# A split-precision decoder trunk: the activation's two parts meet the weight's high part in one 512-column matmul

## The chip, the cores and the metric

The kernel runs on one core of one Trainium2 chip. The metric is the device time of one execution in microseconds (us). A change of about 1% (some 8 us here) is what a measurement of this kernel can just tell from no change.

## The reference

One sequence of 256 tokens with 1024 features goes through two layers. Layer 0 mixes tokens with RWKV-7 time mixing, layer 1 with native sparse attention (compressed, selected and sliding-window branches); each is followed by a dense MLP with a squared ReLU. Everything is float32.

```
def squared_relu_mlp(x, w1, w2):
    return jnp.square(jax.nn.relu(x @ w1)) @ w2          # 1024 -> 4096 -> 1024

for i in range(DEPTH):                                   # DEPTH = 2
    xn = rms_norm(h, mix_norm[i])
    y = rwkv7_time_mix(xn, ...) if i % 2 == 0 else nsa_mix(xn, ...)
    h = h + y                                            # y ends in "@ w_out", 1024 -> 1024
    h = h + squared_relu_mlp(rms_norm(h, mlp_norm[i]), mlp_w1[i], mlp_w2[i])
```

## The kernel before

Activations are held transposed: features on the 128 partitions, 256 tokens (T) along the free axis, eight tiles of 128 features (FT). A dense layer is computed in float32r, the one-pass form of a float32 matmul, which keeps fewer bits of its operands. To keep accuracy every operand is split in two: the weight `raw` into `whi` (its rounded part) and `wlo` (the rest), the activation into a high and a low tile (`xh`/`xl`, `yh`/`yl`, `hh`/`hl`). Three of the four products are added in PSUM: whi times high, whi times low, wlo times high.

Weights are streamed from HBM in 188 units of 512 KB. A unit holds four tiles of 128 input features by 256 output features (`UE` = 1024 values per partition), and lies in one of four slots (`RING`). Each unit goes through four steps:

1. SyncE issues its DMA into `raw` once the slot's former unit has been split (`load`, and the loops in `mlp_loads`).
2. ScalarE copies `raw` to `whi` (`split`, line 1124; `split_of`, line 1359), once TensorE is done with the slot (`unit_used`).
3. VectorE subtracts, `raw` - `whi` gives `wlo` (`rest`, line 1530, reached through `ahead` as well).
4. TensorE runs `unit_mm` (line 454): per input tile k three products, for each of the unit's two output tiles m, so 24 matmuls of 128x128 weights and 256 columns. Output tiles m = 0 and 1 lie in two neighbouring PSUM banks.

Two units make a group, which is a complete result of 256 output features when the layer has 1024 inputs (`a2` and `b2`, with 4096 inputs, take eight units to a group). Groups alternate between banks 0-1 and banks 2-3, so a bank pair has to be emptied before the second next group (`group_free`).

The dense layers, in the order in which they run, are `r`, `k`, `v` (inputs of RWKV, 8 units each), `o0` (its output, 8), `a1` and `a2` (MLP of layer 0, 32 each), `kc`, `ks`, `q`, `vv` (inputs of attention, 20 in all), `o1` (8), `b1` and `b2` (MLP of layer 1, 32 each). The order of the instructions on each engine is the order of the Python code; nothing is rescheduled.

How groups are emptied, in the layers that the change touches:

- `o0`, `a2`, `o1`, `b2`: VectorE adds a bank pair to the residual stream, `h += ps` (`add_residual`, line 1566). Where a norm follows (`residual`), ScalarE then writes `xh` (line 1156) and VectorE `xl` (line 1573) for the next layer, and both gather the squares (`sqn`, lines 1159 and 1579). The next layer's first unit can start while the last two feature pairs are being made: `parts` lets it wait for each pair by itself. After the first group of `a1` or `b1` TensorE takes the mean of the squares (`mean_pe`, line 494), ScalarE its root, VectorE the reciprocal `ri`.
- `a1`, `b1`: VectorE computes `rl` = max(ps, 0) times `ri` (line 1867), which frees the banks; ScalarE squares it into `hh` (line 1363), VectorE squares it into `s2` (line 1870), splits the next two units (line 1530, twice), and writes `hl` = `s2` - `hh` (line 1877). `mlp_dve` and `mlp_act` hold this turn, 16 of them in each MLP.

At the end TensorE transposes `h` (line 1100) and two DMAs store it.

## Time and profile before

| | us |
|---|---|
| median of 3 runs | 777.41 |
| the runs | 769.60, 777.41, 778.11 |
| profiled execution, its own time | 770.58 |
| span of the profiled execution | 768.5 |
| TensorE busy, matmuls | 740.7 (96%) |
| TensorE busy, weight loads | 695.2 (90%) |
| VectorE busy | 520.1 (68%) |
| ScalarE busy | 379.2 (49%) |

The span runs from the first to the last recorded instruction; the profiled execution took 2.1 us more. PE is TensorE's matmuls, PEld its weight loads, which overlap the matmuls, DVE is VectorE, ACT ScalarE, POOL GpSimd, SP SyncE. The duration of one matmul or weight load in a row is its latency; since such instructions overlap, the rate is read from the distance between starts. A true float32 matmul shows as two records (two passes), a float32r one as one record. In "x2" rows of a timeline two equal instructions are merged.

### The profile page before, as it was taken

Reading aid. Unit: us, or ns where it says so; the run is one execution under the profiler, and the core shown is the slowest. Engines: PE = TensorE matmul, PEld = TensorE weight load, DVE = VectorE, ACT = ScalarE, POOL = GpSimd, SP = SyncE. Lnnn points to the kernel's source line nnn. Section 1 sums busy time; section 2 is a strip of 40 time slices with the busy share of each in tenths; the row PEclk is TensorE's granted clock in tenths of the full one; section 3 lists DMA queues with packets and bytes.
Section 4 is the critical chain, followed back from the end, with each engine's and each line's share of the span. In section 5 each row is a group of like instructions: output and inputs, shape, how many; then the busy total and the mean of one; then the engine's idle time right before and its main releaser. Section 6 shows DMA issues by size and latency. Waiting matters only on the chain.

```text
span 768.5 us, 18778 instructions
## 1 busy us (share of the span) xinstructions
PE 740.7 (96%) x7940; PEld 695.2 (90%) x7940; DVE 520.1 (68%) x742; ACT 379.2 (49%) x584; POOL 70.5 (9%) x50
## 2 busy tenths in 40 slices
PE   7999999998999999999999999988899999999997
PEld 6988888997879999999999989866589999999997
DVE  4896985677453788785555678687858887864441
ACT  6656453211443545544444435668866544543341
POOL 0000005190130000000000010024420000000000
PEclk9999999999999999999999999999999999999999
DMA  9854330000111589967666553500045666676551
GB/s 294 272 174 137 96 101 26 5 3 2 58 57 55 165 233 237 241 191 225 193 197 193 169 165 112 164 1 2 1 147 166 203 196 191 191 218 194 191 165 55
DMA packets 110894, 109.24 MB, mean 142 GB/s; under 512 B 7120, under 2 KB 109776, under 8 KB 110704
## 3 DMA queue, kind: packets, MB, share of 16 engines
q1 hardware_dynamic: 110832, 108.34, 46.9%
q8 instruction: 48, 0.79, 0.4%
q14 instruction: 14, 0.11, 0.0%
HBM read 107.28 MB, written 1.05 MB: 141 GB/s over the span
## 4 chain that ended last, share of the span: by engine, by line
PE 84%; DVE 8%; SPq 2%; ACT 2%; DMA 1%; issue 1%; POOL 1%; ACTq 0%; DVEq 0%; POOLq 0%
PE ps L454 64%; PE ps L670 4%; DMA raw<-in_rwkv_w_in 1%; DVE Gs L1715 1%; DVE SB L2057 1%; PE ps L767 1%; PE ps L982 1%; PE ps L569 1%; PE ps L971 1%; PE ps L1001 1%; PE ps L756 1%; DVE nmx L2063 1%; DVE LT L1741 1%; PE ps L552 1%; POOL t L2126 1%
## 5 line engine op out<-in xcount | busy, mean ns | idle before, releaser
L1530 DVE TENSOR_TENSOR wlo<-raw,whi 128x1024 fp32r<-128x1024 f32 x188 | 226.1, 1225 | 88.8 <-ACT whi L1124 86.5
L1124 ACT ACTIVATE whi<-raw 128x1024 fp32r<-128x1024 f32 x124 | 130.3, 1058 | 128.1 <-PE ps L454 122.4
L454 PE MATMUL ps<-xh,whi 128*128 128x256 f32 x896 | 178.1, 280 | 2.7 <-DVE wlo L1530 1.1
L454 PE MATMUL ps<-xl,whi 128*128 128x256 f32 x896 | 175.4, 277 | 0.0
L454 PE MATMUL ps<-xh,wlo 128*128 128x256 f32 x896 | 175.2, 277 | 0.0
L454 PEld LDWEIGHTS ps<-xh,whi 128*128 128x128 f32 x896 | 135.4, 188 | 6.8 <-issue 4.3
L454 PEld LDWEIGHTS ps<-xl,whi 128*128 128x128 f32 x896 | 135.5, 188 | 0.0
L454 PEld LDWEIGHTS ps<-xh,wlo 128*128 128x128 f32 x896 | 135.4, 188 | 0.0
L1359 ACT ACTIVATE whi<-raw 128x1024 fp32r<-128x1024 f32 x64 | 68.0, 1063 | 78.0 <-PE ps L454 59.2
L454 PE MATMUL ps<-hl,whi 128*128 128x256 f32 x512 | 99.8, 276 | 0.0
L454 PE MATMUL ps<-hh,whi 128*128 128x256 f32 x512 | 99.6, 276 | 0.0
L454 PE MATMUL ps<-hh,wlo 128*128 128x256 f32 x512 | 99.6, 276 | 0.0
L454 PEld LDWEIGHTS ps<-hl,whi 128*128 128x128 f32 x512 | 77.2, 188 | 0.0
L454 PEld LDWEIGHTS ps<-hh,whi 128*128 128x128 f32 x512 | 77.0, 188 | 0.0
L454 PEld LDWEIGHTS ps<-hh,wlo 128*128 128x128 f32 x512 | 77.0, 188 | 0.0
L1867 DVE SCALAR_TENSOR_TENSOR rl<-ps,ri 128x512 f32<-128x512 f32 x32 | 22.1, 691 | 30.3 <-PE ps L454 29.9
L670 PEld LDWEIGHTS ps<-DP,LT 64*64 64x64 f32 x1024 | 30.7, 135 | 3.8 <-DVE DP L1746 2.6
L670 PE MATMUL ps<-DP,LT 64*64 64x64 f32 x1024 | 31.8, 219 | 1.9 <-DVE DP L1733 0.9
L2176 POOL TENSOR_TENSOR SB<-SB,cof 128x512 f32<-128x512 f32 (+1 forms) x16 | 24.4, 1524 | 78.3 <-DVE cof L2079 78.1
L1566 DVE TENSOR_TENSOR h<-h,ps 128x512 f32<-128x512 f32 x16 | 11.0, 688 | 29.6 <-PE ps L454 27.1
L1288 ACT ACTIVATE DP<-ps 128x512 f32<-128x512 f32 x16 | 9.6, 597 | 35.8 <-PE ps L670 35.8
L1870 DVE TENSOR_TENSOR s<-rl 128x512 f32<-128x512 f32 x32 | 22.2, 692 | 1.1
(308 smaller groups left out, 974.6 us busy)
## 6 DMA issues: line engine op xcount, KB each, us to landing
raw<-in_mlp_w SPq DMA_DIRECT2D x128, 512.0 KB, 4.5
raw<-in_rwkv_w_in SPq DMA_DIRECT2D x24, 512.0 KB, 5.1
raw<-in_nsa_w_in SPq DMA_DIRECT2D x20, 512.0 KB, 4.7
raw<-in_rwkv_w_out SPq DMA_DIRECT2D x8, 512.0 KB, 3.4
raw<-in_nsa_w_out SPq DMA_DIRECT2D x8, 512.0 KB, 3.5
cw<-in_nsa_cmp_w SPq DMA_DIRECT2D x4, 512.0 KB, 9.1
cst<-in_consts SPq DMA_DIRECT2D x1, 1047.0 KB, 11.3
xtok<-in_x SPq DMA_DIRECT2D x2, 512.0 KB, 4.2
```

Of the source, the lines that this page charges most:

```text
L454: last = mm(ps[:, bank0 + m, 0:T], w[:, slot, c0:c0 + P], x_[:, kk, :], start=(kk == 0 and n == 0), stop=(kk == ktiles - 1 and n == 2))
L552: last = mm(ps[:, 4 + 2 * (k % 2) + i, 0:T], lup[half, k * P:(k + 1) * P], hwa[half, :], start=True, stop=True)
L569: last = mm(ps[0:width, bank, 0:T], ldown[:, k, c0:c0 + width], mixg[:, k, :], start=(k == 0), stop=(k == FT - 1))
L670: last = mm(ps[at(e), bank, p * C:(p + 1) * C], lhs[s][at(e), p, :], DP[s][at(e), p, which, :], start=True, stop=True)
L1124: A(whi[:, s, :], raw[:, s, :], ACT.Copy).then_inc(hi_ready, 1)
L1288: A(dst, ps[:, bank, :].rearrange("p (k n) -> p k n", n=C), ACT.Copy).then_inc(sem(f"inv_act{s}"), 1)
L1359: A(whi[:, 2 * gg + j, :], raw[:, 2 * gg + j, :], ACT.Copy).then_inc(hi_ready, 1)
L1530: v.tensor_tensor(wlo[:, slot, :], raw[:, slot, :], whi[:, slot, :].bitcast(f32), ALU.subtract)\
L1566: v.tensor_tensor(h[:, 2 * g:2 * g + 2, :], h[:, 2 * g:2 * g + 2, :], ps[:, 2 * (g % 2):2 * (g % 2) + 2, 0:T], ALU.add).then_inc(ev_dve, 1)
L1867: v.scalar_tensor_tensor(rl[:, gg, :, :], ps[:, 2 * gg:2 * gg + 2, 0:T], 0.0, normal(2), ALU.max, ALU.mult)\
L1870: v.tensor_tensor(s2[:, gg, :, :], rl[:, gg, :, :], rl[:, gg, :, :], ALU.mult).then_inc(sem("s2_ready"), 1)
L2176: g.tensor_tensor(x, x, cof[:, q, b, 4 * j:4 * j + 4].unsqueeze(2).broadcast_to([P, 4, w]), ALU.mult)\
```

## The change

The high and the low tile of an activation now lie in one tile with an axis of two (`xw`, `yw`, `hw`), at the addresses that they had. For the layers in `WIDE` (`o0`, `a1`, `a2`, `o1`, `b1`, `b2`: 144 of the 188 units) the two products with `whi` become one matmul of 512 columns, high tokens in columns 0-255 and low tokens in columns 256-511 of the bank. `wlo` times high is added to columns 0-255 as before. A unit then has 16 matmuls: 8 of 512 and 8 of 256 columns. The two halves of a bank have to be added when it is emptied: `add_residual` adds one half and then the other; in `a1` and `b1` ScalarE copies the upper half (`lower_sum`), VectorE adds it to the lower (`s1`), and then takes the maximum and the product with `ri`. There ScalarE also squares into `s2` and copies `s2` to `hh`, where VectorE squared before, and VectorE's first split of a turn moves ahead of the emptying. The layers `r`, `k`, `v`, `kc`, `ks`, `q` keep the three products, and `vv` has a function of its own that is not touched.

```
+    WIDE = ("o0", "a1", "a2", "o1", "b1", "b2")
...
-                    for n, (w, x_) in enumerate(((whi, hi), (whi, lo), (wlo, hi))):
+                    if wide:
                         for m in range(2):
                             c0 = k * GW + m * P
-                            last = mm(ps[:, bank0 + m, 0:T], w[:, slot, c0:c0 + P], x_[:, kk, :],
-                                      start=(kk == 0 and n == 0), stop=(kk == ktiles - 1 and n == 2))
+                            mm(ps[:, bank0 + m, :], whi[:, slot, c0:c0 + P], both[:, :, kk, :],
+                               start=first, stop=end, skip_group_check=True)
+                            last = mm(ps[:, bank0 + m, 0:T], wlo[:, slot, c0:c0 + P], both[:, 0, kk, :],
+                                      start=False, stop=end, skip_group_check=True)
+                        continue
...
+                def low_sum(i, gg):
+                    act.wait_ge(unit_used, i * 4 + (U0[n1] + 2 * gg + 2))
+                    A(lower_sum[:, gg, :, :], ps[:, 2 * gg:2 * gg + 2, T:2 * T], ACT.Copy).then_inc(sem("low_out"), 1)
+
                 def square(i, gg):
-                    act.wait_ge(ev_dve, i * 2 + (EV0[n1] + gg + 1))
-                    A(hh[:, ds(i * 4 + 2 * gg, 2), :], rl[:, gg, :, :], ACT.Square).then_inc(sem("hh_ready"), 1)
+                    act.wait_ge(sem("rl_ready"), i * 2 + (base_ + gg + 1))
+                    A(s2[:, gg, :, :], rl[:, gg, :, :], ACT.Square).then_inc(sem("s2_ready"), 1)
+                    act.wait_ge(sem("s2_ready"), i * 2 + (base_ + gg + 1))
+                    A(hh[:, ds(i * 4 + 2 * gg, 2), :], s2[:, gg, :, :], ACT.Copy).then_inc(sem("hh_ready"), 1)
...
                 with act.Fori(1, 8) as i:
                     for gg in range(2):
                         split_of(i, gg, 0)
+                        low_sum(i, gg)
                         split_of(i, gg, 1)
                         square(i, gg)
...
             def add_residual(res, g):
-                v.tensor_tensor(h[:, 2 * g:2 * g + 2, :], h[:, 2 * g:2 * g + 2, :],
-                                ps[:, 2 * (g % 2):2 * (g % 2) + 2, 0:T], ALU.add).then_inc(ev_dve, 1)
+
+                part = h[:, 2 * g:2 * g + 2, :]
+                banks = slice(2 * (g % 2), 2 * (g % 2) + 2)
+                step(v.tensor_tensor(part, part, ps[:, banks, T:2 * T], ALU.add))
+                settle()
+                v.tensor_tensor(part, part, ps[:, banks, 0:T], ALU.add).then_inc(ev_dve, 1)
...
                 def turn(i, gg):
+                    u = U0[n1] + 2 * gg + RING
+                    rest(2 * gg, i * 4 + (u + 1))
                     dve.wait_ge(unit_used, i * 4 + (U0[n1] + 2 * gg + 2))
-                    v.scalar_tensor_tensor(rl[:, gg, :, :], ps[:, 2 * gg:2 * gg + 2, 0:T], 0.0, normal(2), ALU.max, ALU.mult)\
-                        .then_inc(ev_dve, 1)
+                    dve.wait_ge(sem("low_out"), i * 2 + (base_ + gg + 1))
+                    v.tensor_tensor(s1[:, :, :], lower_sum[:, gg, :, :], ps[:, 2 * gg:2 * gg + 2, 0:T], ALU.add).then_inc(ev_dve, 1)
                     dve.wait_ge(ev_dve, i * 2 + (EV0[n1] + gg + 1))
-                    v.tensor_tensor(s2[:, gg, :, :], rl[:, gg, :, :], rl[:, gg, :, :], ALU.mult).then_inc(sem("s2_ready"), 1)
-                    for j in range(2):
-                        u = U0[n1] + 2 * gg + j + RING
-                        rest(2 * gg + j, i * 4 + (u + 1))
+                    v.scalar_tensor_tensor(rl[:, gg, :, :], s1[:, :, :], 0.0, normal(2), ALU.max, ALU.mult)\
+                        .then_inc(sem("rl_ready"), 1)
+                    rest(2 * gg + 1, i * 4 + (u + 2))
 
                     dve.wait_ge(sem("hh_ready"), i * 2 + (base_ + gg + 1))
-                    dve.wait_ge(sem("s2_ready"), i * 2 + (base_ + gg + 1))
                     v.tensor_tensor(hl[:, ds(i * 4 + 2 * gg, 2), :], s2[:, gg, :, :],
                                     hh[:, ds(i * 4 + 2 * gg, 2), :].bitcast(f32), ALU.subtract).then_inc(sem("hid_ready"), 1)
```

How TensorE's instructions stand in the loop over the groups of `a1`, first before and then after the change (`wboth` holds `whi` and `wlo`, `hw` holds `hh` and `hl`; line 454 became lines 461 and 463). The piece of before is the start of a unit in `a1`, the piece of after that of a unit in `a2`; both layers run the same function:

```order
L866 REGISTER_ALU
L454 MATMUL ps<-xh_58,whi 128x256 [waits lo_ready]
L454 MATMUL ps<-xh_58,whi 128x256
L454 MATMUL ps<-xl_60,whi 128x256 x2
L454 MATMUL ps<-xh_58,wlo 128x256 x2
L454 MATMUL ps<-xh_58,whi 128x256 x2
```

```order
L891 REGISTER_ALU
L461 MATMUL ps<-hw,wboth 128x512 [waits lo_ready]
L463 MATMUL ps<-hw,wboth 128x256
L461 MATMUL ps<-hw,wboth 128x512
L463 MATMUL ps<-hw,wboth 128x256
L461 MATMUL ps<-hw,wboth 128x512
```

Of six matmuls per input tile four are left, and successive ones now go to the same bank in pairs.

VectorE's turn in `a1`, of before and then of after (`s_130` and `s_125` are `s2`, `s_127` is `s1`, line 1530 became 1553, `hl` a part of `hw`):

```order
L1867 SCALAR_TENSOR_TENSOR rl<-ps,ri 128x512 [waits unit_used]
L1869 REGISTER_ALU
L1870 TENSOR_TENSOR s_130<-rl 128x512 [waits ev_dve]
L1529 REGISTER_ALU
L1530 TENSOR_TENSOR wlo<-raw,whi 128x1024 [waits hi_ready]
```

```order
L1553 TENSOR_TENSOR wboth<-raw,wboth 128x1024 [waits hi_ready]
L1895 REGISTER_ALU
L1896 ISA [waits unit_used]
L1897 TENSOR_TENSOR s_127<-lower_sum,ps 128x512 [waits low_out]
L1898 REGISTER_ALU
L1899 SCALAR_TENSOR_TENSOR rl<-s_127,ri 128x512 [waits ev_dve]
L1552 REGISTER_ALU
L1553 TENSOR_TENSOR wboth<-raw,wboth 128x1024 [waits hi_ready]
L1904 ISA [waits hh_ready]
L1904 TENSOR_TENSOR hw<-s_125,hw 128x512
```

The banks are freed by line 1897, which stands behind one split and waits for ScalarE's copy; VectorE has five long instructions in a turn as before.

ScalarE's turn in `a1` after the change:

```order
L1374 ACTIVATE wboth<-raw 128x1024 [waits unit_used]
L1377 REGISTER_ALU
L1378 ACTIVATE lower_sum<-ps 128x512 [waits unit_used]
L1374 ACTIVATE wboth<-raw 128x1024 [waits unit_used,raw_in1]
L1381 ISA
L1382 ACTIVATE s_125<-rl 128x512 [waits rl_ready]
```

The copy of the upper half stands between the two splits; line 1384, the copy to `hh`, follows. Before the turn was split, split, square.

## Rows read from the trace of the kernel before

**Rows 1.** The page: busy shares, granted clock by slices, chain by engine.
```profile
PE 740.7 (96%) x7940; PEld 695.2 (90%) x7940; DVE 520.1 (68%) x742; ACT 379.2 (49%) x584; POOL 70.5 (9%) x50
...
PEclk9999999999999999999999999999999999999999
...
PE 84%; DVE 8%; SPq 2%; ACT 2%; DMA 1%; issue 1%; POOL 1%; ACTq 0%; DVEq 0%; POOLq 0%
```

**Rows 2.** Chain that ended last, in order of time: start, length, what.
```profile
235.65 28.51 PE ps L454 x240
265.02 174.11 PE ps L454 x1536
...
593.15 168.67 PE ps L454 x1488
```

**Rows 3.** Timeline at 437.5 us: start, length, engine, line, instruction.
```profile
437.49 0.30 PEld L454 LDWEIGHTS ps<-xh,whi 128*128 128x128 f32 x2
437.60 0.39 PE L454 MATMUL ps<-xh,whi 128*128 128x256 f32 x2
437.72 0.30 PEld L454 LDWEIGHTS ps<-xl,whi 128*128 128x128 f32 x2
437.83 0.39 PE L454 MATMUL ps<-xl,whi 128*128 128x256 f32 x2
```

**Rows 4.** Weight loads grouped by form: busy, mean ns, idle before.
```profile
L454 PEld LDWEIGHTS ps<-hl,whi 128*128 128x128 f32 x512 | 77.2, 188 | 0.0
...
L1001 PEld LDWEIGHTS ps<-PT,vt 128*64 128x64 f32 x96 | 5.5, 135 | 4.2 <-issue 2.5 <-ACT PT L1473 0.6
```

**Rows 5.** Eight passes of 64 columns with 128x128 weights, timeline.
```profile
489.35 1.06 PE L932 MATMUL ps<-cw,hpad 128*128 128x64 f32 x8
```

**Rows 6.** Line 606, eight passes of 512 columns, and the weight load inside it.
```profile
L606 PE MATMUL ps<-t,cst x8: 590/592/592, 107.9 to 110.9; 128*128 128x512 f32 x8
...
108.34 0.19 PEld L606 LDWEIGHTS ps<-t,cst 128*128 128x128 f32 x1 [0.24 <-issue]
```

**Rows 7.** Layer `vv`: float32r matmuls one after another into one bank.
```profile
490.42 0.28 PE L952 MATMUL ps<-wlo,xh 128*128 128x256 f32 x1
490.53 0.28 PE L953 MATMUL ps<-whi,xl 128*128 128x256 f32 x1
...
492.91 0.28 PE L953 MATMUL ps<-whi,xl 128*128 128x256 f32 x1
```

**Rows 8.** Splitting and emptying, grouped by form: busy, mean ns, idle before.
```profile
L1530 DVE TENSOR_TENSOR wlo<-raw,whi 128x1024 fp32r<-128x1024 f32 x188 | 226.1, 1225 | 88.8 <-ACT whi L1124 86.5 <-DVE mixw L1553 0.6 <-DVE BK L1682 0.4
...
L1359 ACT ACTIVATE whi<-raw 128x1024 fp32r<-128x1024 f32 x64 | 68.0, 1063 | 78.0 <-PE ps L454 59.2 <-DMA raw<-in_mlp_w 18.7
...
L1867 DVE SCALAR_TENSOR_TENSOR rl<-ps,ri 128x512 f32<-128x512 f32 x32 | 22.1, 691 | 30.3 <-PE ps L454 29.9 <-DVE ri L1588 0.5
L1877 DVE TENSOR_TENSOR hl<-s,hh 128x512 f32 x32 | 21.9, 685 | 0.0
L1363 ACT ACTIVATE hh<-rl 128x512 f32 x28 | 17.2, 613 | 0.0
```

**Rows 9.** Timeline from the last matmuls of `o0` to the mean in `a1`.
```profile
258.34 0.40 PE L454 MATMUL ps<-xh,whi 128*128 128x256 f32 x2
258.59 0.69 DVE L1566 TENSOR_TENSOR h<-h,ps 128x512 f32<-128x512 f32 x1 [1.36 <-issue]
260.71 0.88 DVE L1573 SCALAR_TENSOR_TENSOR xl<-h,par,xh 128x256 fp32r<-128x256 f32 x2
262.65 0.68 DVE L1579 TENSOR_TENSOR sqn<-sqn 128x512 f32<-128x512 f32 x1
263.99 1.02 PE L494 MATMUL ps<-sqn,cst 128*128 128x256 f32 x4
```

**Rows 10.** Timeline of the end.
```profile
761.85 0.69 DVE L1566 TENSOR_TENSOR h<-h,ps 128x512 f32<-128x512 f32 x1 [8.50 <-PE ps L454]
762.59 1.07 PEld L1100 LDWEIGHTS ps<-cst,h 128*128 128x128 f32 x10 [0.36 <-DVE h L1566]
```

**Rows 11.** Stretches: length, busy PE, PEld, DVE, ACT, POOL, clock, DMA share, GB/s.
```profile
250.00:300.00 50.00, 50.00 (x435) 49.89 (x434) 40.66 (x52) 26.20 (x33) 0.00 (x0) 1.00 0.77 211
300.00:350.00 50.00, 50.00 (x444) 50.00 (x443) 39.35 (x47) 24.32 (x28) 0.00 (x0) 1.00 0.81 217
```

62 lines of the change are left out of this document (36 added, 26 removed).

## The prediction

> **What bounds the kernel now.** Start with the page: matmuls fill 96% of the span, the chain that ended last is TensorE for 84%, and the granted clock is at full speed (2.4 GHz) in all 40 slices [rows 1]. The chain in order of time then shows where TensorE never pauses: 1536 dense matmuls in one piece of 174.11 us, 1488 in one of 168.67 us [rows 2]. No wait for VectorE, ScalarE or a DMA breaks them. So in the layers `a1` to `b2` only the time per matmul counts: (174.11 - 0.28) / 1535 = 113.2 ns, and the same from the other piece. From 235.65 to 264 us (all of `o0` and the first two units of `a1`) the same instruction comes every (28.51 - 0.28) / 239 = 118.1 ns; why it is slower there no row tells.
>
> The next question is what makes 113.2 ns, since the change removes instructions but no columns. 256 columns at 2.4 GHz are 106.7 ns; 6.5 ns are something else. Three groups bear on it.
> - The timeline of a dense layer: the weight load of a matmul starts one step (0.11 us) before its matmul, so it runs beside the matmul ahead of it [rows 3]. In line 606 too a load starts at 108.34, when a matmul of 0.43 us starts, and the next load only after 0.24 us of idling [rows 6]. So one load can be ahead, not two.
> - A load of 128 columns shows 188 ns and one of 64 shows 135: (188 - 135) / 64 = 0.83 ns per column, so 128 columns occupy the loader for about 106 ns beyond a fixed latency [rows 4]. That is as long as a stream of 256 columns.
> - Where there is hardly anything to stream, the load shows its own rate: line 932 runs eight passes of 64 columns on 128x128 weights in 1.06 us [rows 5]; less a latency of about 0.28 us, that is 0.78 / 7 = 112 ns a pass, nearly the 113.2 of the dense layers, with a quarter of the columns.
> So I read the dense layers as bound by the weight load, by a hair. Where the load is hidden, the stream has little overhead: the passes of line 606 start 3.0 / 7 = 429 ns apart for 512 columns of true float32, which is 0.419 ns per column and half-pass, so 214 ns for 512 columns and 107 ns for 256 [rows 6].
>
> The Trainium skill, page "TensorE: Matmul & The Clock Gate", section "Back-to-back issue gap", gives a warm gap of N / 2.4 + 2.5 ns, so 109.2 ns for 256 columns and 215.8 for 512. The trace does not agree for 256 (113.2); by that rule with nothing else in play the change would save 2.5 ns for each of the 1152 matmuls that go, 2.9 us, and the result would be no change. That is rival 1 with a smaller constant.
>
> **The change part by part.**
> 1. *Matmuls.* A pair of 256-column matmuls on the same `whi` becomes one of 512; it occurs 8 times in a unit, in 144 units. Not seen in the trace is a float32r matmul of 512 columns. From below it is 214 ns (line 606). From above it is 226.4, twice a narrow one: then nothing is gained. I take 216: the load of its successor (112) is well hidden under it, and a few ns remain for the float32r form. The narrow `wlo` matmul behind it runs beside the load for the next wide one and stays at 113.2. A pair then saves 2 x 113.2 - 216 = 10.4 ns; in the 134 units at 113.2, 134 x 8 x 10.4 = 11.1 us; in the 10 units at 118.1 (80 pairs), 80 x 20.2 = 1.6 us. Sum 12.7 us.
> 2. *The same bank twice in a row.* In `vv` all three products go to one bank one after another, and they start (492.91 - 490.42) / 22 = 113.2 ns apart [rows 7]. So this costs nothing.
> 3. *Emptying in `a1` and `b1`.* A group lasts 2 x 8 x (216 + 113.2) = 5.27 us (before 5.43). With the durations of rows 8 the turn, run freely, is a ring: ScalarE's split 1.06, VectorE's split 1.23, s1 0.69, rl 0.69, ScalarE's square 0.61 and copy 0.61, then its next split. That is 4.89, with six handovers of about 0.04 us some 5.1 us, under the 5.27. (ScalarE's copy of the upper half, 0.6, and its second split lie beside VectorE's part.) VectorE alone has 2 x 1.2 + 3 x 0.69 = 4.5. The banks are free about 0.6 + 0.7 + handovers = 1.4 us after a group ends, and wanted after 5.27. A slot: ScalarE's second split starts 0.7 us after the group's end, its `wlo` is done at 3.4, the reload lands some 5 us later, and the slot is wanted again at 10.5. Nothing reaches TensorE; cost 0. If the cover went, a turn of p us would cost (p - 5.27) x 16 for each MLP beyond a slack of 3.9 us. DMA carries 211 to 217 GB/s at a share of 0.77 to 0.81 in `a1` [rows 11]; 3% more fits. ScalarE waited 18.7 us for weights there [rows 8] and TensorE did not feel it; the first split of a turn now ends earlier, so reloads start earlier.
> 4. *Two adds instead of one* (0.69 and a wait for itself, 0.75 us more), 16 groups. It counts only where someone waits for the last group:
>    - `o0` to `a1`: `o0` ends at about 258.34; the add is over 0.94 us later, the last `xl` at 261.59, the sum of squares at 263.33, while TensorE takes the mean at 263.99, having 48 matmuls to run [rows 9]. Now the squares are ready at +5.74 and the units done at +5.27, so TensorE stands for 0.5 us and a handover: 0.6 us. The last `xl` (+4.0) meets the matmul that wants it at 1.5 units (+3.95): contained in this.
>    - `o1` to `b1`: the same instructions, with the squares 0.1 us later in relation: 0.7 us.
>    - `a2` to `kc`: `kc` keeps its 24 matmuls a unit and has a margin of about 1 us: 0.
>    - the end: the transposes wait for the add [rows 10]: 0.75 us.
>    Sum 2.05 us. The other 12 groups have another whole group's time of cover.
> 5. *What does not move:* addresses, loads, the other 44 units.
>
> Sum: -12.7 + 2.05 = -10.7 us. Against the profiled execution of 770.6 that is 759.9. The executions shown are 769.6, 770.6, 777.4 and 778.1, in two clusters that no row explains; which one the next median meets is open, so I set the sum against their mean, 773.9: 763. In the lower cluster I expect 759 to 760, in the upper 766 to 767.
>
> **Rivals.**
> 1. *The 6.1 ns beyond the stream belong to every matmul, not to the load* (113.2 against 107). Then a wide one takes 214 + 6 = 220.4, a pair saves 6.1 ns: 1072 x 6.1 + 80 x 11 = 7.4 us, less 2.05 = 5.4 us. 765 in the lower cluster, 768.5 against the mean. For it: 118.1 ns in `o0`, which a fixed load time doesn't explain. Against it: line 932's 112 ns with 64 columns, line 606 with hardly any surplus. Chance 0.22.
> 2. *Loads get two ahead under the long matmul,* so that the narrow one runs at its stream's 107: a pair of matmuls takes 321 instead of 340 (354 in `o0`): 1072 x 18.5 + 80 x 33 = 22.5, less 2 = 20.5 us, 750 to 753. Against it: the idle 0.24 us of the loader in rows 6. Chance 0.06.
> 3. *Slower: the turn in `a1` and `b1` becomes the bound.* ScalarE and VectorE now hand over six times in a ring that has only 0.15 us to spare. If a handover costs 0.2 instead of 0.04, or the copy waits behind a late weight (rows 8 show such waits), a turn takes 6.2 us: 32 x 0.93 - 7.8 = 22 us lost (7.8 is the slack of 3.9 in each MLP), 760 + 22 = 782 in the lower cluster, 785 against the mean. It decides from 5.85 us a turn (32 x 0.58 - 7.8 = 10.8, break-even); a turn of 5.6 eats 2.8 us only. For it: how close the ring is; against it: a single slow turn is forgiven by two groups of bank slack, and the rows' own handovers are short. Chance 0.07.
> 4. *The load is exposed, and fewer loads save it whole.* If each load took its 106 ns beside no matmul, 8 fewer in a unit would save 144 x 8 x 106 ns = 122 us: 650. Rows 3 speak against it: 113 ns have no room for 107 of stream and 106 of load. Chance 0.01. The Trainium skill, same page, section "Part 3: Packing small matmuls", says of loads that they overlap with matmuls in flight only when the row group differs; the trace does not agree: both use all 128 rows here, and they overlap.
> Forecast 0.64.
>
> **How the numbers follow.** Faster by over 1% (7.7 us, about what a measurement can tell): most of the forecast (0.64, less 0.05 for its lower edge) and rivals 2 and 4 (0.07): 0.66. Within 1%: rival 1 and that edge: 0.27. Slower: rival 3: 0.07. The range: from 751 (rival 2 in the lower cluster) to 773 (rival 1 in the upper cluster: 778.1 - 5.4). It leaves out rival 3, rival 4, and little else.
>
> **What would show it.** In the profile after, steps between matmuls of a unit alternate 216 and 113 ns (a group 5.27 us). Rival 1: 220 and 113, rival 2: 214 and 107. The chain's long pieces stay unbroken in `a1` and `b1`; rival 3 would show PE idle behind s1 or `wlo`. Before both `mean_pe` TensorE waits about 0.6 us for `sqn`, and the last transposes wait 0.75 us longer. Weight loads drop in share (16 for 24), far below 90%. I am wrong if the wide matmul is above 222 ns, or if PE stands still inside `a1`.

## The result, and the profile after

| | before | after |
|---|---|---|
| median, us | 777.76 (4 runs, 769.60 to 779.48) | 786.36 (4 runs, 785.06 to 787.66) |
| profiled execution, its own time | 770.58 | 786.16 |
| its span | 768.5 | 784.1 |

The changed kernel is slower: ratio 1.016, 95% interval 1.0109 to 1.0211 (the two medians alone divide to 1.011). It was predicted at 763 in a range of 751 to 773, faster. Ratios and intervals in this document leave out a run that is over 1.5% above the quickest of the same kernel; medians and ranges include it. The profiled execution of before is one of its quickest; the two spans differ by 15.6 us, and that difference is what has to be explained.

The page of after, the lines that answer to [rows 1]:

```profile
PE 756.0 (96%) x6788; PEld 656.4 (84%) x6788; DVE 535.5 (68%) x758; ACT 414.2 (53%) x648; POOL 70.4 (9%) x50
...
PEclk9999999999999999999999999989999999999999
...
PE 87%; DVE 8%; ACT 2%; issue 1%; DMA 1%; POOL 1%; ACTq 0%; SPq 0%; DVEq 0%; POOLq 0%
```

1152 matmuls and as many weight loads are gone (6788 for 7940), the loader's share fell from 90% to 84%, and yet TensorE is busy 15.3 us *longer* (756.0 for 740.7). The granted clock is as it was, one slice apart, and it is at full speed (1.00) in the stretches of `a1` and `b1` that were read. So the time went into TensorE's own columns. How fast they go is read from starts in the timeline of `a1`, TensorE and its loader alone (compare [rows 3]):

```profile
302.14 0.40 PE L461 MATMUL ps<-xw,wboth 128*128 128x512 f32 x1
302.37 0.28 PE L463 MATMUL ps<-xw,wboth 128*128 128x256 f32 x1
302.38 0.19 PEld L461 LDWEIGHTS ps<-xw,wboth 128*128 128x128 f32 x1
302.49 0.40 PE L461 MATMUL ps<-xw,wboth 128*128 128x512 f32 x1
302.49 0.19 PEld L463 LDWEIGHTS ps<-xw,wboth 128*128 128x128 f32 x1
302.73 0.28 PE L463 MATMUL ps<-xw,wboth 128*128 128x256 f32 x1
```

From wide to narrow 0.235 us, from narrow to the next wide 0.118: a pair takes 0.353 us where three narrow ones took 3 x 0.1132 = 0.340. Over the eight pairs of a unit and the 134 units that had been at 113.2 ns that is 134 x 8 x 13.6 ns = 14.6 us. Read piece by piece from the starts of the two executions it is 14.3 us: 6.8 in `a1` and `a2` (with 0.2 of it in the first group of `kc`, which is narrow and now went at 117.7 behind the wide stream), 6.6 in `b1` and `b2`, 0.9 in `o1`. The transitions (below) add 1.3, and what else moved in the kernel comes to 0.1. In words: before, 256 columns took 113.2 ns in the long stretches of [rows 2]; after, they take 117.8 ns in the layers changed, be it in a wide or in a narrow matmul.

Does anything make TensorE stand still inside `a1`? ScalarE's turn in the timeline shows that the emptying is not late:

```profile
298.80 0.60 ACT L1378 ACTIVATE lower_sum<-ps 128x512 f32<-128x512 f32 x1 [1.22 <-PE ps L463]
...
300.88 0.63 ACT L1382 ACTIVATE s<-rl 128x512 f32<-128x512 f32 x1 [0.54 <-DVE rl L1899]
...
304.46 0.60 ACT L1378 ACTIVATE lower_sum<-ps 128x512 f32<-128x512 f32 x1 [1.22 <-PE ps L463]
```

One turn is 304.46 - 298.80 = 5.66 us, which is 16 pairs of 0.353; and in each ScalarE waits 1.22 us for TensorE's last narrow matmul. So it is from the fifth turn on; 24 of the 32 copies wait for TensorE. In the first turns, where ScalarE and VectorE have the start of the layer to catch up with, the copies follow one another without a wait, at 272.12, 276.99 and 281.95 us: run freely, a turn takes 4.9 to 5.0 us (the prediction had 5.1). TensorE's matmuls keep their step there too. The ring has room; TensorE sets the pace.

The transitions, from the timeline of after (the answers to [rows 9] and [rows 10]):

```profile
263.43 0.28 PE L463 MATMUL ps<-xw,wboth 128*128 128x256 f32 x1
263.72 1.13 PE L509 MATMUL ps<-sqn,cst 128*128 128x256 f32 x4
...
776.80 0.69 DVE L1592 TENSOR_TENSOR h<-h,ps 128x512 f32<-128x512 f32 x1 [8.93 <-PE ps L463]
777.52 0.69 DVE L1594 TENSOR_TENSOR h<-h,ps 128x512 f32<-128x512 f32 x1
778.26 1.31 PE L1115 MATMUL ps<-cst,h 128*128 128x128 f32 x10 [0.84 <-DVE h L1594]
```

Before the mean TensorE loses 263.72 - 263.43 less one step of 0.12, which is 0.17 us (the same before the mean of `b1`, from 600.09 to 600.38), and the second add at the end takes 777.52 - 776.80 = 0.7 us: together 1.0. Each mean is itself 0.11 us longer (1.13 for 1.02 in [rows 9]), which makes it 1.3.

Three questions remain. Why does a wide matmul take 235 ns and not 216? Why did the narrow ones go from 113.2 to 117.8? And are the two clusters in the times of before the same thing?

### The profile page after: what moved, and what is told of

Same layout as the page of the kernel before. It is cut to its first block, busy times and chain, and to the rows that moved or that the text cites. A ratio compares the mean times of both kernels' runs of the same rounds, so it can differ in the third digit from the quotient of the medians.

```text
span 784.1 us, 16566 instructions
## 1 busy us (share of the span) xinstructions
PE 756.0 (96%) x6788; PEld 656.4 (84%) x6788; DVE 535.5 (68%) x758; ACT 414.2 (53%) x648; POOL 70.4 (9%) x50
## 4 chain that ended last, share of the span: by engine, by line
PE 87%; DVE 8%; ACT 2%; issue 1%; DMA 1%; POOL 1%; ACTq 0%; SPq 0%; DVEq 0%; POOLq 0%
PE ps L461 35%; PE ps L463 17%; PE ps L469 15%; PE ps L685 4%; DVE SB L2084 1%; DVE Gs L1742 1%; PE ps L782 1%; PE ps L584 1%; ACT SB L1485 1%; DVE nmx L2090 1%; PE ps L986 1%; PE ps L997 1%; PE ps L771 1%; DVE LT L1768 1%; DMA xtok<-in_x 1%
## 5 line engine op out<-in xcount | busy, mean ns | idle before, releaser
L1553 DVE TENSOR_TENSOR wboth<-raw,wboth 128x1024 fp32r<-128x1024 f32 x188 | 228.9, 1226 | 92.0 <-ACT wboth L1139 87.0
L461 PE MATMUL ps<-xw,wboth 128*128 128x512 f32 x576 | 204.2, 398 | 1.6 <-DVE xw L2112 1.0
L1139 ACT ACTIVATE wboth<-raw 128x1024 fp32r<-128x1024 f32 x124 | 130.2, 1057 | 128.5 <-PE ps L463 112.2
L461 PE MATMUL ps<-hw,wboth 128*128 128x512 f32 x512 | 181.0, 397 | 0.0
L463 PE MATMUL ps<-xw,wboth 128*128 128x256 f32 x576 | 161.9, 281 | 0.0
L463 PE MATMUL ps<-hw,wboth 128*128 128x256 f32 x512 | 143.9, 281 | 0.0
L461 PEld LDWEIGHTS ps<-xw,wboth 128*128 128x128 f32 x576 | 108.3, 188 | 28.8 <-issue 2.2
L469 PE MATMUL ps<-xw,wboth 128*128 128x256 f32 x960 | 116.8, 281 | 0.8 <-ACT R L1212 0.7
L469 PEld LDWEIGHTS ps<-xw,wboth 128*128 128x128 f32 x960 | 112.5, 188 | 4.4 <-issue 2.1
L461 PEld LDWEIGHTS ps<-hw,wboth 128*128 128x128 f32 x512 | 96.3, 188 | 23.8
L463 PEld LDWEIGHTS ps<-xw,wboth 128*128 128x128 f32 x576 | 108.1, 188 | 0.1
L463 PEld LDWEIGHTS ps<-hw,wboth 128*128 128x128 f32 x512 | 96.1, 188 | 0.0
L1374 ACT ACTIVATE wboth<-raw 128x1024 fp32r<-128x1024 f32 x64 | 67.1, 1049 | 0.0
L1904 DVE TENSOR_TENSOR hw<-s,hw 128x512 f32 x32 | 22.2, 693 | 16.1 <-ACT hw L1384 16.1
L1897 DVE TENSOR_TENSOR s<-lower_sum,ps 128x512 f32<-128x512 f32 x32 | 21.9, 685 | 13.0 <-ACT lower_sum L1378 13.0
```

The source lines that it names most:

```text
L461: mm(ps[:, bank0 + m, :], whi[:, slot, c0:c0 + P], both[:, :, kk, :], start=first, stop=end, skip_group_check=True)
L463: last = mm(ps[:, bank0 + m, 0:T], wlo[:, slot, c0:c0 + P], both[:, 0, kk, :], start=False, stop=end, skip_group_check=True)
L469: last = mm(ps[:, bank0 + m, 0:T], w[:, slot, c0:c0 + P], both[:, part, kk, :], start=(first and n == 0), stop=(end and n == 2))
L1139: A(whi[:, s, :], raw[:, s, :], ACT.Copy).then_inc(hi_ready, 1)
L1374: A(whi[:, 2 * gg + j, :], raw[:, 2 * gg + j, :], ACT.Copy).then_inc(hi_ready, 1)
L1553: v.tensor_tensor(wlo[:, slot, :], raw[:, slot, :], whi[:, slot, :].bitcast(f32), ALU.subtract)\
```

## The experiments

The recorded expectations name the theories by letters; they are said here where they come up first. Runs of before that are quoted beside an experiment were made on the same chip in between. None leaves a part of the computation out; what some add is said.

**1. Before, once more.** No edit. Theory A: the two clusters of before are the two steps that [rows 2] show, 118 and 113 ns, held through a whole stream of matmuls.

> The kernel before, once more, unchanged, for a second profile of it. In its first profile the dense matmuls of 256 columns run in one of two steps, 117.8 ns or 113.3 ns, and change from one to the other only where the dense stream is broken. Theory A (two steps of the stream, drawn anew at each start of a stream): this execution may have another pattern; if the layers a1/a2 or b1/b2 hold 117.8 ns throughout, the execution takes about 1500 x 4.5 ns = 7 us longer for each, which would be the cluster at 777 us. Theory B (the step is fixed by what the code does at that place): the pattern is the same in every execution, 265 us on at 113.3, and the clusters come from elsewhere.

This execution took 777.18 us (span 775.1), which is the upper cluster. Its chain in order of time, to be laid beside [rows 2]:

```profile
234.62 28.50 PE ps L454 x240
263.98 180.91 PE ps L454 x1536
...
599.78 168.68 PE ps L454 x1488
```

`a1` and `a2`: (180.91 - 0.28) / 1535 = 117.7 ns, where the other execution of the same program had 113.2. `b1` and `b2`: 113.3 in both. The piece is 6.8 us longer, and the two executions differ by 6.6. `o1` was slower as well, 25.68 us for 24.75. So A holds for this pair: the narrow stream has two steps, and one is taken at the start of a stream and kept, 1536 matmuls long. The fact stood in [rows 2] as 118.1 against 113.2. It is not the clock, which was fully granted at either step; compare this stretch at 117.7 ns with the same one in [rows 11] (427 matmuls here, 444 there):

```profile
300.00:350.00 50.00, 50.00 (x427) 50.00 (x426) 37.45 (x45) 23.36 (x27) 0.00 (x0) 1.00 0.81 211
```

The clusters stand out when the 70 later runs of before are laid beside the mean granted clock of each run, which lies between 0.985 and 0.995. At 0.993 the times are 769.0 to 770.3 or 776.5 to 776.9; at 0.990 they are 769.3 to 772.1 or 777.4 to 779.2; at 0.988 they are 771.9 to 774.2 or 778.3 to 780.2. In each there are two groups some 7 us apart, and 775.38 at 0.986 is the only time that could belong to either. So the clock makes the spread inside a cluster, and the gap between the clusters has the size of one long stream at the slower step. That it is this stream in every run was seen in two traces only.

**2. Two narrow matmuls for each wide one,** with the changed emptying kept.

```
-                            mm(ps[:, bank0 + m, :], whi[:, slot, c0:c0 + P], both[:, :, kk, :],
-                               start=first, stop=end, skip_group_check=True)
+                            mm(ps[:, bank0 + m, 0:T], whi[:, slot, c0:c0 + P], both[:, 0, kk, :],
+                               start=first, stop=False, skip_group_check=True)
+                            mm(ps[:, bank0 + m, T:2 * T], whi[:, slot, c0:c0 + P], both[:, 1, kk, :],
+                               start=False, stop=end, skip_group_check=True)
```

> The changed kernel, but each matmul of 512 columns is two of 256 (whi times high into columns 0-255, whi times low into columns 256-511 of the same bank). Order of banks, emptying, ScalarE's and VectorE's turns stay as in the changed kernel. Theory 1 (the 512-column form is what runs at 235.5 ns, that is 117.8 for 256 columns): the steps go back to 113.3 ns in a1 and a2 and the kernel takes that of before plus about 2 us, 771 to 773 us in its lower cluster. Theory 2 (the order of banks, or ScalarE's and VectorE's new work, slows the stream): the steps stay at 117.8 ns and the time at 785 to 788 us.

770.96 us in the profiled execution, span 768.9, and 113.3 ns in `a1` to `b2`. Everything of the change but the width of the matmul stands in this kernel, and it can be as quick as before was: the emptying is not the cause. But this was the quickest of 10 runs. The others took 776.61 to 786.66, the median was 780.17 and the ratio 1.0088 (1.0045 to 1.0131). By their times, seven runs have one long stream at the slower step and two runs (786.19 and 786.66) both; no trace of those was taken. Two theories are left for that, how a stream starts and which banks follow one another (experiments 7 and 11).

**3. Each shape by itself.** Behind `b2`, when all other engines have nothing to do, a block of matmuls is run in several shapes, twice (results unused). Theory S: the stream of columns sets the time. L: the weight load does, as I had predicted. G: what costs is the operand in two pieces far apart. C: other engines' work slows the stream.

```
+                for n in range(20):
+                    mm(ps[:, 4 + n % 2, :], wgt(n), hw[:, :, n % 16, :], start=True, stop=True)
+                for n in range(20):
+                    mm(ps[:, 4 + n % 2, :], wgt(n), hw[:, 0, 2 * (n % 8):2 * (n % 8) + 2, :], start=True, stop=True)
+                for n in range(40):
+                    mm(ps[0:64, 4 + n % 2, 0:T], wgt(n, 64), hw[:, 0, n % 16, :], start=True, stop=True)
+                for n in range(40):
+                    mm(ps[:, 4 + n % 2, 0:P], wgt(n), hw[:, 0, n % 16, 0:P], start=True, stop=True)
...
```

> The changed kernel, with blocks of extra matmuls behind b2, when no other engine works; their results are not used. Each block twice: 256 columns; 512 (two runs of 256) and 256 in turn as in the changed kernel; the same with 512 neighbouring columns; 512 alone in both forms; 256 columns with 64 columns of weights; 128 and 64 columns with 128x128 weights; 512 columns of true float32. Theory L (the weight load bounds the narrow matmul, the stream is free at 0.417 ns a column): 256 columns 113 ns, 128 and 64 columns 112 ns as well, 256 columns with 64 weight columns 107 to 109 ns, 512 alone 214 to 216 ns. Theory S (float32r streams at 0.46 ns a column, or 0.4425 when narrow): 512 alone 235.5 ns, 256 with 64 weight columns 113 to 118 ns, 128 columns well under 112 ns. Theory G (two separate runs of 256 columns in the moving operand cost it): the block with 512 neighbouring columns is at 216 ns and the other at 235 ns. Theory C (VectorE and ScalarE disturb the stream in the changed kernel): every block is faster here than in the layers.

The chain of this kernel, by blocks: wide with two pieces (L1123), wide with neighbouring columns (L1125), 256 columns with half the weight columns (L1127), 128 columns (L1129), and a true float32 matmul (L1133):

```profile
799.05 4.67 PE ps L1123 x20
803.72 4.67 PE ps L1125 x20
808.39 4.76 PE ps L1127 x40
813.15 4.41 PE ps L1129 x40
...
823.25 19.33 PE ps L1133 x40
```

- Wide alone: 4.67 / 20 = 233.5 ns, in two pieces or in one. From start to start they take 231 and 236 ns by turns. G falls.
- Half the weight columns: 119 ns for 256 columns. A shorter load saves nothing, so 256 columns are not bound by the load. L falls, and with it the reason for 216.
- 128 columns: 110 ns on the mean; the block of 64 columns steps at 112 ns while the clock is fully granted. Half the columns save nothing, so here the load is the bound. Theory S had put 128 columns well under 112. That this rate lies so near 113 misled me in [rows 5].
- No other engine was at work and the times are those of the kernel. C falls.

S is left: a float32r matmul takes 0.44 to 0.46 ns per column, whether the columns come in one instruction or in two. True float32 (429 ns per record, here and in [rows 6], once the clock is fully granted; the mean of 483 includes a start at half clock) moves at another rate per column and could not stand for it.

**4. Another order: two wide, then two narrow.** The wide and narrow matmuls stand in separate loops over m.

```
                               start=first, stop=end, skip_group_check=True)
+                        for m in range(2):
+                            c0 = k * GW + m * P
                             last = mm(ps[:, bank0 + m, 0:T], wlo[:, slot, c0:c0 + P], both[:, 0, kk, :],
```

> The changed kernel, with the two 512-column matmuls of a tile first (bank m = 0, then m = 1) and the two 256-column ones behind them, so that successive matmuls alternate banks as before the change. Theory B (two matmuls in a row into one bank cost the fast step): 2 x 113.3 to 216 ns for a wide one, 113.3 for a narrow one, 769 to 773 us. Theory S (a 512-column float32r matmul takes 235.5 ns wherever it stands, and the narrow one next to it 117.8): unchanged, 785 to 788 us.

The timeline at 300 us, TensorE alone:

```profile
300.63 0.62 PE L461 MATMUL ps<-xw,wboth 128*128 128x512 f32 x2
301.10 0.39 PE L465 MATMUL ps<-xw,wboth 128*128 128x256 f32 x2
301.33 0.62 PE L461 MATMUL ps<-xw,wboth 128*128 128x512 f32 x2
```

The second wide matmul of the pair that starts at 300.63, by itself:

```profile
300.86 0.40 PE L461 MATMUL ps<-xw,wboth 128*128 128x512 f32 x1
```

Two wide and two narrow take 0.693 us where two pairs take 0.707: 115.5 ns per 256 columns. From start to start (300.63, 300.86, 301.10) the first wide one takes 226 ns and the second 236, the narrow ones 118 and 113. So a wide matmul can go at the quick rate, 226 = 2 x 113, and in this order every second one does, 246 of 493 in `a1` and `a2`. 10 runs: median 779.12 (776.88 to 780.12), ratio 1.0074 (1.0036 to 1.0111). Neither theory had named this time. The order alone is worth some 8 us against after on the same chip (787.22, experiment 5), and still it loses to before.

**5. After, once more.** No edit.

> The changed kernel again, unchanged, for its spread beside that of before on the same chip. If each dense stream of the changed kernel draws one of two steps as the kernel before does, its times spread over two or three clusters 7 us apart (771, 778, 786). If the 512-column form knows only the slow step, all lie within 785 to 788 us while those of before spread over 769 to 779.

Median 787.22, 786.38 to 788.04 in 4 runs, ratio 1.0206 (1.0143 to 1.0269). Before spread by 13 us on the same chip (768.76 to 781.64), after by 2: in its order it has only the one step.

**6. A short matmul at the start of each group of before,** 88 in all, of true float32 with 64 columns (result unused). Theory K: what stands just ahead of a stream chooses its step (for a true float32 matmul the expectation calls it F).

```
                     for j in range(2):
...
+                            if j % 2 == 0:
+                                mm(ps[:, 7, 0:64], cc("ident"), cc("chunk")[:, 0:64], start=True, stop=True)
```

> The kernel before, with one true-float32 matmul of 64 columns (into an unused bank, result unused) ahead of each unit in a1 and b1 from the third group on and ahead of every second unit in a2 and b2: 88 of them, each at most 0.12 us, so at most 10 us. Theory D (the step is drawn anew whenever the float32r stream is broken): the profile shows stretches at 113.3 and at 117.8 ns within one layer, changing at these places, and the clusters merge into times between. Theory F (a true-float32 matmul always leads to the fast step, as behind the mean in the first profile): all stretches at 113.3 ns. Theory P (the step is fixed for a layer from outside): one step throughout each layer as in the kernel before.

The timeline around one of them:

```profile
301.80 0.39 PE L454 MATMUL ps<-xh,wlo 128*128 128x256 f32 x2
302.03 0.33 PE L867 MATMUL ps<-cst 128*128 128x64 f32 x2
302.17 0.48 PE L454 MATMUL ps<-xh,whi 128*128 128x256 f32 x2
302.49 0.40 PE L454 MATMUL ps<-xl,whi 128*128 128x256 f32 x2
```

All stretches behind such matmuls were at 113.3 ns from the fifth matmul on, as K says. But each costs about 0.24 us (I had allowed 0.12 at most): 88 x 0.24 = 21 us, and the median was 793.07 (790.14 to 794.53), ratio 1.0273 (1.0204 to 1.0342). As a repair it is dearer than the fault.

**7. What stands ahead of a stream, measured by itself.** Behind `b2`, five times over: 32 narrow matmuls behind a short true float32 one, behind two long ones, behind a short float32r one, behind a wide float32r one; then 16 wide ones (results unused).

```
+            for rep in range(5):
+                mm(ps[:, 6, 0:64], cc("ident"), cc("chunk")[:, 0:64], start=True, stop=True)
+                stream(32)
+                for n in range(2):
+                    mm(ps[:, 6 + n, 0:T], cc("ident"), cc("chunk"), start=True, stop=True)
+                stream(32)
+                mm(ps[:, 6, 0:64], wgt(rep), hw[:, 0, 0, 0:64], start=True, stop=True)
+                stream(32)
+                mm(ps[:, 6, :], wgt(rep), hw[:, :, 0, :], start=True, stop=True)
+                stream(32)
```

> The changed kernel, with streams of 32 narrow float32r matmuls (or 16 of 512 columns) behind b2, when no other engine works, five times each behind: one true-float32 matmul of 64 columns; two of 256; one float32r of 64 columns; one float32r of 512. Theory D (drawn at each start): each kind shows both steps, 113.3 and 117.8 ns, over its five repetitions. Theory K (the kind of what stands before decides): a kind shows one step in all five; in the changed kernel kc followed a wide stream at the fast step, so the kind behind a 512-column float32r would be fast. The 512-column streams: 2 x 113.3 at times under theory D, always 233 to 236 ns under theory S (the wide form knows only the slow step).

The chain, one repetition (streams of 32 are L1116, the two of 16 wide ones L1120):

```profile
802.75 3.70 PE ps L1116 x32
...
807.31 3.77 PE ps L1116 x32
811.08 0.03 PE ps L1128
811.12 3.73 PE ps L1116 x32
...
815.07 3.77 PE ps L1116 x32
...
819.00 3.79 PE ps L1120 x16
```

3.70 and 3.73 us behind a short one, 3.77 behind a long one; the mean record of a matmul is 276 ns in the quicker streams and 281 in the others. The lengths lie close together because a short one ahead makes the first steps of its stream longer (200 ns for the first); after that the steps are 113.3 ns behind a short one and 117.8 behind a long one. It came out the same five times of five, so here the step was not chance. Behind a wide float32r one the stream was slow, where K had expected it quick. The wide streams took 3.79 and 3.81 us, 237 ns each with their start, and step at 231 and 236 ns by turns as in experiment 3: no short matmul makes them quicker.

**8 to 10. Seven short float32r matmuls,** one at the start of each long stream (`r`, `k`, `v`, `o0`, `o1`, and the second group of `a1` and `b1`; result overwritten), in before (8), in the kernel of experiment 2 (9) and in after (10).

```
+                    if short and k == 0:
+                        mm(ps[:, bank0 + 2 - 4 * (bank0 // 2 % 2) if kbase else bank0, 0:64], whi[:, slot, 0:P], hi[:, kk, 0:64], start=True, stop=True)
```

> The kernel before, with one float32r matmul of 64 columns (overwritten or unused result) at seven starts of a dense stream: ahead of r, k, v, o0, of the second group of a1 and of b1, and of the second unit of o1. Theory K (what stands ahead of a float32r stream sets its step; behind 64 columns it is 113.3 ns, behind 256 or 512 it is 117.8 or what it was): o0, a1, a2, b1 and b2 run at 113.3 ns in every execution, the upper cluster is gone, and all times lie at 767 to 771 us, 7 x 0.14 us of cost included. Theory D (drawn by chance): the clusters at 770 and 777 us stay.

> The same seven short matmuls in the kernel that has the changed emptying and two matmuls of 256 columns in place of each of 512. With the step held at 113.3 ns in both, the difference to e8 is the price of the changed emptying alone: 2.05 us by the prediction's sum, so 769 to 773 us in one cluster. If ScalarE's and VectorE's longer turn reaches TensorE in a1 or b1, it is more, and TensorE stands still there.

> The same seven short matmuls in the changed kernel. Theory S (a 512-column float32r matmul followed by one of 256 takes 353.3 ns whatever stands ahead of the stream): 785 to 788 us as without them. Theory K2 (the wide form too has a fast step, which the changed kernel never met because no short matmul stood ahead): a pair at 340 ns, 770 to 773 us.

| | median, us | runs | ratio, 95% |
|---|---|---|---|
| 8, before | 771.22 | 11, 769.37 to 772.96 | 0.9955, 0.9919 to 0.9991 |
| 9, experiment 2 | 772.31 | 11, 771.00 to 781.24 | 0.9998, 0.9957 to 1.0038 |
| 10, after | 787.91 | 5, 786.95 to 789.02 | 1.0188, 1.0130 to 1.0246 |

In experiment 8 all dense layers from `o0` on went at 113 ns, as its chain shows:

```profile
235.22 27.29 PE ps L456 x240
263.41 174.18 PE ps L456 x1536
```

`o0` and the first units of `a1` took 27.29 us where before took 28.51. No run of the 11 lies in the upper cluster, where 11 of the 21 runs of before beside it do. Seven of the times lie above the 767 to 771 that K had named, by up to 2 us. Experiment 10 is the clean one: the same short matmuls ahead of the wide and narrow pairs left them at 117.8 but for a few at the starts of streams (span 785.1). The alternation took no quicker step. Experiment 9 has seven of its 11 times at 771 to 773, but its profiled execution (778.86) had `o1`, `a1` and `a2` at 117.8: against K, the short matmul doesn't hold it there always.

**11. Order and banks apart.** Behind `b2` six blocks, four times over, each behind a short matmul in the first and third round and behind a wide one in the others (results unused). Theory W: a wide and a narrow one in turn have the slow step whatever the bank. B: it is the same bank twice running that costs.

```
+                    for n in range(8):
+                        if block == 0:
+                            wide_(4, n), wide_(5, n), slim(4, n), slim(5, n)
+                        if block == 1:
+                            wide_(4, n), slim(4, n), wide_(5, n), slim(5, n)
+                        if block == 2:
+                            wide_(4, n), slim(5, n, True), wide_(5, n), slim(4, n, True)
+                        if block == 3:
+                            slim(4, n), slim(4, n), slim(4, n), slim(5, n), slim(5, n), slim(5, n)
+                        if block == 4:
+                            slim(4, n), slim(5, n), slim(4, n), slim(5, n), slim(4, n), slim(5, n)
+                        if block == 5:
+                            wide_(4, n), wide_(4, n), wide_(4, n)
```

> The changed kernel, with six blocks of float32r matmuls behind b2, each eight times the work of three times two 256-column matmuls, behind a 64-column matmul (first and third repetition) or a 512-column one (second and fourth): (1) wide bank 4, wide bank 5, narrow 4, narrow 5; (2) wide 4, narrow 4, wide 5, narrow 5; (3) wide 4, narrow 5, wide 5, narrow 4; (4) narrow three times on one bank, then on the other; (5) narrow, banks in turn; (6) wide only, one bank. A block holds 48 times 256 columns: 5.44 us at 113.3 ns, 5.65 us at 117.8. Theory W (the change of width costs, not the bank): (2) and (3) 5.65, (1) 5.55, (6) 5.6, in both kinds of repetition; (4) and (5) 5.44 behind the short and 5.65 behind the long one. Theory B (the bank decides): (3) is as (1).

The chain, the first round (block 1 of the code is at 784 to 790 us, block 2 at 790 to 796), and at the end blocks 3 and 4 of the second round:

```profile
780.64 0.46 PE ps L1113 x2
781.10 0.23 PE ps L1114 x2
781.34 0.46 PE ps L1113 x2
...
785.28 0.23 PE ps L1113
785.63 0.23 PE ps L1113
...
792.09 0.23 PE ps L1113
792.44 0.23 PE ps L1113
...
795.65 5.73 PE ps L1114 x48
801.41 5.54 PE ps L1114 x48
...
830.45 5.66 PE ps L1114 x48
836.34 5.45 PE ps L1114 x48
```

Two and two: 0.693 us for four, with the steps of experiment 4 (226 and 236 ns, 118 and 113). In turn: 0.353 for a pair, in the same bank (785.28 to 785.63) and in another (792.09 to 792.44). So the order in which wide and narrow follow one another counts and the bank does not: W holds and B falls for the wide ones. For narrow ones alone W had said that the matmul ahead decides, and that failed. Three in a row to one bank took 5.73 and 5.66 us for 48 (118 to 119 ns), banks in turn 5.54 and 5.45 (114 to 115, start included), behind either kind of matmul. Neither the bank nor the matmul ahead is a rule, though. The layer `vv` [rows 7] and the profile of experiment 2 have three or more in a row to one bank at 113.3 ns. And experiment 7 has narrow ones with banks in turn at 117.8 ns behind a wide one, where such a stream steps at 113.3 here.

**12. Experiment 9 with the banks in turn:** the three narrow products of before's order, but in both halves of the bank, so that only the emptying of the change is left.

```
+                        for n, (w, part, at_) in enumerate(((whi, 0, 0), (whi, 1, T), (wlo, 0, 0))):
+                            for m in range(2):
+                                c0 = k * GW + m * P
+                                last = mm(ps[:, bank0 + m, at_:at_ + T], w[:, slot, c0:c0 + P], both[:, part, kk, :],
+                                          start=first and n == 0, stop=end, skip_group_check=True)
```

> As e9 (seven short matmuls, the changed emptying, two matmuls of 256 columns for each of 512), but with the six matmuls of an input tile in the order of the kernel before, so that successive ones go to the two banks in turn. Theory T (three in a row into one bank are what let a1 and a2 fall to 117.8 ns in e9's profile): all dense layers at 113.3 ns, one cluster, and the difference to e13 is the price of the changed emptying alone: 1.05 us by the stretches of the changed kernel's trace, so 770 to 774 us. Theory D (chance alone): times of e9, 771 to 781 us.

The chain has `a1` and `a2`, `b1` and `b2` in whole pieces at 113.3 ns:

```profile
265.42 168.75 PE ps L464 x1488
...
594.03 168.76 PE ps L464 x1488
```

Span 770.2 where experiment 8 has 768.4, both with all streams at 113: 1.8 us more with the changed emptying, from two single executions, of which this one had the lower granted clock (0.988 for 0.991). Read at the three transitions alone (before the two means, and behind the last matmul of `b2`) it is 0.3 + 0.3 + 0.7 = 1.4 us. Median 774.59 in 11 runs, ratio 1.0024 (0.9988 to 1.0061). The times reach from 771.02 to 779.14, and one run took 786.65, as much above as two slow streams would make; T had named one cluster. Part of the spread goes with the granted clock, 0.986 to 0.994.

**13. Experiment 8 once more,** to see whether its gain of 0.45% stands.

> e8 once more, beside e12 and the kernel before: if the seven short matmuls hold the fast step, no run lies above 773.5 us, while a third or more of the runs of the kernel before do; ratio 0.993 to 0.998.

Median 773.15 in 12 runs (769.10 to 780.25), ratio 1.0012 (0.9977 to 1.0047). It does not stand. Four runs lie above 773.5, and of before only 5 of 23 did on this chip. In its profiled execution `o1` was at 117.8 in spite of its short matmul, and one run took 780.25. No version here is shown to beat before. The short matmuls did make the upper cluster rare: 1 of 23 runs in experiments 8 and 13 lies there, against 16 of the 44 runs of before beside them. They cost about 1 us (7 x 0.14), and how much they give back depends on how often before meets the slower step, which was 11 of 21 on one chip and 5 of 23 on the other.

## Why the prediction was wrong, point by point

- **The step that failed is part 1, "I take 216".** It rested on reading 113.2 ns as the weight load's time. Experiment 3 gives 119 ns with half the load, so the load was covered all along. What was predicted at 216 measured 235.5 in the kernel and 233.5 alone; the quickest that any wide one took is 226 (experiments 4 and 11). Even the upper end, 226.4, "then nothing is gained", was no bound: it doubled the quicker of two steps. The test that the prediction set itself, a wide matmul above 222 ns, came out against it.
- **The narrow matmul "stays at 113.2": wrong.** Next to a wide one it takes 117.8 (after, experiments 10 and 11). Of the 13.6 ns lost in a pair, 235.5 - 226.4 = about 9 are the wide one's and 4.6 the narrow one's.
- **Where the reading went astray.** Line 932 [rows 5] has few columns and shows the load's rate, 110 to 112 ns; that it came near 113.2 was a coincidence that I took for a cause. Line 606 [rows 6] is another number form. And the row that spoke against both, 118.1 ns for the same instruction in [rows 2], was put aside with "no row tells". No load time explains two rates for one instruction; it was reason enough for a wider range.
- **Rival 1** (a fixed 6.1 ns for each matmul) is wrong too: the surplus goes with the columns, not with the matmuls, or 512 would have taken 220. Rivals 2 and 4, in which fewer loads pay, fall with the load.
- **Rival 3** said 785 and the time was 786, but not by its mechanism: ScalarE waits 1.2 us for TensorE in a turn of `a1` once it has caught up, and a turn run freely takes 4.9 to 5.0 us. A number that fits is no confirmation; the wait that it named isn't there.
- **Part 2** (one bank several times in a row costs nothing) was read from `vv` at 113.2 and holds for the pairs, which are as slow with other banks. For narrow ones three in a row it held in experiment 2's profile and not in experiment 11, which has 118 to 119 there against 114 to 115.
- **Part 3** was right and **part 4** too high. Nothing of the emptying reached TensorE inside `a1`, with groups of 5.66 us; the 5.27 that the prediction reckoned with never came up, but the free turn of 4.9 to 5.0 us is below it. The waits before the means were 0.17 us each where 0.6 and 0.7 were worked out. That fits the slower group before the mean, which gave the squares 5.66 us instead of 5.27 (5.74 - 5.66 and a handover). The end cost 0.7 (0.75). In all 1.0 us, 1.3 with the longer means, instead of 2.05; experiment 12, whose groups were quick, has 1.4.
- **The clusters** "that no row explains" have the size of what a row I had shows: 1536 or 1488 matmuls at one step or the other, about 7 us each time. Against the median of before, 777.76, which by that count has one of its two long streams at 118, the change loses 8.6 us; against the profiled execution 15.6. That reading rests on two profiled executions and on the times of the others (experiment 1).

What stays open: why a float32r stream has two steps, and what chooses. A short matmul ahead gave the quick one in experiment 6, in all five repetitions of experiment 7 and in experiment 8; in `o1` and `a1` of experiment 9 and `o1` of experiment 13 it did not, and in experiment 11 the step was the same whatever stood ahead. Ahead of `a1` before has the same four matmuls of the mean in every execution, and yet it went at 113.2 ns in one and at 117.7 in the other. Why a wide and a narrow one in turn keep to the slow rate is open as well; experiment 11 shows that they do, and that two and two do not, but not why. Widths between 256 and 512 were not tried.

## What to carry to other kernels

Where TensorE never pauses, count columns at the measured rate of that number form, and don't expect time back for fewer matmuls or fewer weight loads until a stream with a shorter load has been measured and is quicker. A price for a shape that the trace doesn't have is worth a block of 20 such matmuls behind the kernel's end before anything is rewritten. And when runs of one kernel fall into clusters, lay their times beside the granted clock of each run, and compare the step between matmuls stretch by stretch in two executions: what differs there may be as large as the change.

## What the runs showed of the hardware that was not expected

- A float32r matmul of 256 columns on 128x128 weights has two steps, 113.3 and 117.7 ns, at the same granted clock, with or without other engines at work (experiments 1 and 7). One is taken at a stream's start and can hold for 1536 matmuls.
- A wide one takes 226, 231 or 236 ns, the sums of two quick, of a quick and a slow, and of two slow steps of 256 columns: 235.5 in turn with a narrow one, 231 and 236 by turns when alone (mean 233.5), 226 and 236 when two wide stand before two narrow. Columns in one piece or in two made no difference.
- Weight loads of 128 columns are covered from 256 columns on (64 weight columns: 119 ns); at 128 and at 64 columns of stream they are the bound, at 110 to 112 ns (experiment 3).
- A true float32 matmul of 64 columns inside a float32r stream costs 0.24 us, while its two passes of 64 columns at the 0.42 ns per column of [rows 6] would be 0.05. A short float32r one in experiment 7 costs 0.14 us: a piece of 0.03 of its own, and 0.1 in the longer steps behind it.
- With 64 columns for each load the granted clock fell. These stretches of experiment 3 are the block of 64 columns before and after the fall (length, busy PE, PEld, DVE, ACT, POOL, clock, DMA share, GB/s):

```profile
818.00:820.40 2.40, 2.40 (x24) 2.40 (x23) 0.00 (x0) 0.00 (x0) 0.00 (x0) 1.00 0.00 0
820.60:823.00 2.40, 2.40 (x13) 2.40 (x13) 0.00 (x0) 0.00 (x0) 0.00 (x0) 0.50 0.00 0
```

The clock goes from 2.4 to 1.2 GHz, and the step from 112 to 214 ns. TensorE had run the block of 128 columns until 817.4 us and 64 columns a load since then. It was back at 2.4 GHz in the block of float32 behind it, whose steps go from 854 to 429 ns. What in that change of work makes the clock fall was not tried.
